# Hybrid RG-LRU / attention block on one core: the merge products as seven half-size products, with token sums made by accumulating transfers

## The chip, the core and the metric

The kernel runs on one core of a Trainium2 chip as one program. A core has TensorE (PE, matrix products), VectorE (DVE), ScalarE (ACT), GpSimd (POOL) and SyncE (SP), each with an instruction stream of its own; they meet through semaphores. Data moves by transfers that an engine issues into its own DMA queue and that run on the core's 16 DMA engines. The metric is the device time of one execution in microseconds (us); lower is better.

## The reference, cut to what matters

One layer over 1024 tokens of 1024 channels, all in float32:

```
y_rnn  = h_x * gelu(gx)                      # scan branch, (1024, 1024)
y_na   = neighborhood_attention(...)         # attention branch, (1024, 1024)
merged = sigmoid(g_rnn) * (y_rnn @ w_rnn_out) + sigmoid(g_na) * (y_na @ w_na_out)
x = x + mx[2] * (merged @ w_out)
x = x + mx[5] * conv_ffn(modulate(x, norm_ffn_g, mx[3], mx[4]), w_up, conv_w, conv_b, w_down)
```

`mx` is the modulation, `silu(c) @ w_mod + b_mod`, in six parts of 1024 columns. Parts 0 and 1 go into the first norm, part 2 is the merge's gate, 3 and 4 shift and scale the second norm, 5 is the gate of the last sum.

## The kernel before, in words

Channels lie on the 128 partitions, tokens along the rows; `KC = 8` chunks of 128 channels make up 1024. `HALF` is 512 tokens or columns. A float32 product is made of three passes: each operand is split into a high part (a cast on ACT) and a low part (raw minus high, on DVE), and PE adds high x high, high x low and low x high into a PSUM bank. PE's unit of work is a matmul with 128x128 stationary weights and 128x512 moving tokens.

The stages in order, with their place in the trace:

- Setup, 0 to 94 us.
- Eight mixer turns (`PAIRS = 8`, one per 128 channels and two heads), 140.5 us each: the projections, the scan, the attention. Each turn stores a chunk of the scan branch to `yr_d` (512 KB), four pieces of the attention branch to `yn_d`, and the two gates' sigmoids to `smr_d` and `smn_d`. POOL does the small exchanges (`exchange_low`), the last step of each sigmoid and the bias adds.
- The merge, 1215 to 1472 us: three phases (`w_rnn_out`, `w_na_out`, `w_out`), each with eight units, one per 128 output channels. A unit is 2 halves x 8 chunks x 3 passes = 48 matmuls. ACT and DVE split the unit's 512 KB of weights; the tokens (`ah`, `al`) are held split in SBUF for the whole phase. In phase 1 DVE multiplies by the gate, adds and splits the merged rows for phase 2. POOL loads one row of gates (`aux`) per unit when DVE frees a buffer. Between the units DVE also makes 32 modulation columns (`mod_column`, L1610: one 128x1024 product with a running sum each; L1613 adds the bias). 24 of the 1152 matmuls already run in the last mixer turn (`mix_piece`), where ACT and DVE also split the eight chunks of `yr_d` (`y_high`, `y_low`) and the first two units of weights.
- The tail of the merge and the second norm, to about 1500 us: `last_unit`, `last_step` and `sum_squares`/`spread` are woven so that PE has work while the norm's short chain runs.
- The feed-forward up products to 1912 us, most of them already made as seven half-size products per pair of 1024-wide blocks. POOL makes the sums of weights that these need by transfers that add into DRAM (L2111, `accum_op=ALU.add`; L2113 are its plain copies).
- The down projection, 1912 to 2127 us: 77 steps of 12 matmuls, also as seven products. SP loads each step's weights and tokens eight steps ahead (`STEP_RING = 8`).

The order of the work is written out by hand on each engine; nothing plans it at run time.

## Time and profile before

| | |
|---|---|
| median of 3 runs | 2131.67 us (2128.15 to 2136.17) |
| profiled execution | 2128.76 us, its span 2126.9 us |
| granted TensorE clock | 0.997 |
| PE busy | 2051.1 us (96%), 10618 matmuls |
| DVE busy | 1628.0 us (77%) |
| ACT busy | 1072.5 us (50%) |
| POOL busy | 492.8 us (23%) |
| DMA | 241.65 MB, mean 114 GB/s |

The profile is of one execution. Its page gives busy time by engine, the span in 40 slices (a digit is the busy tenth of a slice), the chain of work that ended last and the costliest groups of instructions. The rows further down come from that page and from views of the same trace: windows (busy time of each engine in a stretch), lines (groups of instructions by source line), sources (one line's instructions, and for transfers the time from issue to landing) and timelines (single instructions, with the idle time before each in square brackets and what ended it).

### The profile page before, as it was taken

What the parts mean: (1) busy time and instruction counts of PE and PEld (TensorE: products, weight loads), DVE (VectorE), ACT (ScalarE), POOL (GpSimd) and SP (SyncE); (2) the same over time, 40 slices, a digit from 0 to 9 for tenths busy, and PEclk for the clock granted to TensorE, in tenths of its full rate; (3) what the DMA queues carried; (4) which work ended last, traced back from release to release, by engine and by line L of the source; (5) the groups of instructions that cost most, each with busy time, mean ns of one, the idle gap of its engine ahead of it and who ended that gap; (6) DMA issues with size and microseconds to landing.
All of it is one profiled execution on the core that took longest, in us unless ns stands there. A gap on an engine that the chain in (4) does not pass through costs nothing.

```text
span 2126.9 us, 28320 instructions
## 1 busy us (share of the span) xinstructions
PE 2051.1 (96%) x10618; PEld 1739.8 (82%) x10618; DVE 1628.0 (77%) x2809; ACT 1072.5 (50%) x1631; POOL 492.8 (23%) x377
## 2 busy tenths in 40 slices
PE   5999999999999999999998899999999999999999
PEld 1878888988988889888887788887788888887887
DVE  6688598596885985859859866767998888877766
ACT  3466666665676657656666621002444334434332
POOL 0031130222212212212123010000124442115550
PEclk9999999999999999999999999999999999999999
DMA  8421211112012120120111385453347764239663
GB/s 328 112 64 41 62 51 47 47 53 70 30 41 72 40 73 20 53 70 30 43 50 69 106 310 193 144 188 131 89 134 197 183 176 118 94 122 335 226 205 126
DMA packets 105576, 241.65 MB, mean 114 GB/s; under 512 B 27264, under 2 KB 32768, under 8 KB 104960
## 3 DMA queue, kind: packets, MB, share of 16 engines
q1 hardware_dynamic: 74304, 191.08, 26.4%
q0 software_dynamic: 14592, 44.05, 8.0%
q10 hardware_dynamic: 16544, 4.72, 1.0%
q8 instruction: 84, 1.38, 0.3%
q14 instruction: 52, 0.43, 0.1%
HBM read 203.11 MB, written 63.96 MB: 126 GB/s over the span
## 4 chain that ended last, share of the span: by engine, by line
PE 77%; DVE 13%; ACT 4%; issue 2%; ACTq 0%; DVEq 0%
PE banks L47 14%; PE banks L49 14%; PE banks L48 14%; PE banks L991 4%; PE banks L862 4%; PE banks L864 4%; PE banks L863 4%; PE banks L895 3%; PE banks L2269 3%; PE banks L2270 3%; PE banks L2271 3%; DVE probT_low L1494 2%; PE banks L953 2%; DVE prob L1486 2%; PE banks L935 1%
## 5 line engine op out<-in xcount | busy, mean ns | idle before, releaser
L47 PE MATMUL banks<-qh,xnh 128*128 128x384 f32 (+1 forms) x640 | 223.3, 349 | 0.3 <-PEq L216 0.3
L862 PE MATMUL banks<-xnh,wh 128*128 128x512 f32 (+1 forms) x536 | 211.3, 394 | 3.2 <-ACT stage L1097 2.9
L49 PE MATMUL banks<-qh,xnl 128*128 128x384 f32 (+1 forms) x640 | 207.7, 325 | 0.0
L48 PE MATMUL banks<-ql,xnh 128*128 128x384 f32 (+1 forms) x640 | 207.6, 324 | 0.0
L864 PE MATMUL banks<-xnh,wl 128*128 128x512 f32 (+1 forms) x536 | 204.5, 381 | 0.0
L863 PE MATMUL banks<-xnl,wh 128*128 128x512 f32 (+1 forms) x536 | 204.1, 381 | 0.0
L1494 DVE TENSOR_TENSOR probT_low<-banks,probT_high 128x512 fp32r<-128x512 f32 (+2 forms) x256 | 138.9, 583 | 56.2 <-ACT probT_high L1165 55.2
L1165 ACT CAST probT_high<-banks 128x512 fp32r<-128x512 f32 (+2 forms) x256 | 117.0, 510 | 60.3 <-PE banks L953 51.4
L47 PE MATMUL banks<-yh,wh 128*128 128x512 f32 x372 | 145.0, 390 | 0.9 <-DVE wl L2471 0.9
L48 PE MATMUL banks<-yl,wh 128*128 128x512 f32 x372 | 145.0, 390 | 0.0
L49 PE MATMUL banks<-yh,wl 128*128 128x512 f32 x372 | 144.9, 390 | 0.0
L1362 DVE TENSOR_REDUCE ssq<-sqs 128x4 f32<-128x256 f32 (+1 forms) x80 | 31.0, 389 | 141.5 <-ACT sqs L1107 141.0
L803 POOL TENSOR_TENSOR stage<-stage,one 128x512 f32<-128x512 f32 x32 | 39.0, 1217 | 417.8 <-ACT stage L1097 417.8
L813 POOL TENSOR_TENSOR rstd<-rstd,power 128x24 f32<-128x24 f32 (+1 forms) x16 | 58.9, 3680 | 312.3 <-DVE rstd L1400 312.3
L2106 POOL TENSOR_TENSOR conv_d<-conv_d 128x1024 f32<-128x1024 f32 x22 | 69.1, 3141 | 262.8 <-ACT conv_d L2340 201.0
L1155 ACT ACTIVATE prob<-prob,stat 128x768 f32<-128x768 f32 (+1 forms) x128 | 128.2, 1002 | 2.5 <-DVE stat L1489 2.5
L47 PEld LDWEIGHTS banks<-qh,xnh 128*128 128x128 f32 x640 | 120.8, 189 | 9.0 <-issue 8.1
L48 PEld LDWEIGHTS banks<-ql,xnh 128*128 128x128 f32 x640 | 120.8, 189 | 8.3 <-issue 7.6
L49 PEld LDWEIGHTS banks<-qh,xnl 128*128 128x128 f32 x640 | 120.7, 189 | 0.0
L1780 ACT CAST wh<-raw 128x1024 fp32r<-128x1024 f32 x22 | 23.2, 1055 | 189.4 <-PE banks L49 158.9
L864 PEld LDWEIGHTS banks<-xnh,wl 128*128 128x128 f32 x536 | 101.3, 189 | 19.7
L862 PEld LDWEIGHTS banks<-xnh,wh 128*128 128x128 f32 x536 | 101.7, 190 | 17.3 <-issue 3.0
(396 smaller groups left out, 6015.9 us busy)
## 6 DMA issues: line engine op xcount, KB each, us to landing
raw<-w_ff SPq DMA_DIRECT2D x33, 512.0 KB, 5.7
down_d<-w_down POOLq DMA_DIRECT2D x66, 256.0 KB, 6.9
raw<-w_fm SPq DMA_DIRECT2D x32, 512.0 KB, 6.7
extras<-h_d SPq DMA_DIRECT2D x55, 256.0 KB, 3.9
raw<-w_qkv SPq DMA_DIRECT2D x24, 512.0 KB, 3.9
raw<-w_mix SPq DMA_DIRECT2D x24, 512.0 KB, 4.8
h_d<-conv_d SPq DMA_DIRECT2D x21, 512.0 KB, 3.2
raw<-w_modT SPq DMA_DIRECT2D x16, 512.0 KB, 4.6
```

Of the source, the lines that this page charges most:

```text
L47: pe.matmul(out, w_hi(k), x_hi(k), start=(k == 0), stop=False)
L48: pe.matmul(out, w_hi(k), x_lo(k), start=False, stop=False)
L49: last = pe.matmul(out, w_lo(k), x_hi(k), start=False, stop=(k == chunks - 1))
L862: pe.matmul(out, fh[:, s, k, :], xnh[:, k, c0:c1], start=(k == 0), stop=False)
L863: pe.matmul(out, fh[:, s, k, :], xnl[:, k, c0:c1], start=False, stop=False)
L864: return pe.matmul(out, fl[:, s, k, :], xnh[:, k, c0:c1], start=False, stop=(k == KC - 1))
L895: pe.matmul(f_bank(j)[:, 0:c1 - c0], lw[:, 2 * (n // 3) + d, :], xc[:, c0:c1], start=True, stop=True).then_inc(f_full, 1)
L991: last = pe.matmul(dst, vS[:, s, h, :], moving, start=(n == 0 and part == 0), stop=(n == len(blocks) - 1 and part == 1))
L1155: act.activation(p, p, ACT.Exp, bias=stat[:, u, 1:2], scale=-1.0, accum_out=stat[:, u, 2:3]).then_inc(exp_done, 1)
L1165: act.copy(probT_blocks(pth, u, bank), probT_bank(u, bank)).then_inc(pt_hi, 1)
L1494: dve.tensor_tensor(probT_blocks(ptl, u, bank), probT_bank(u, bank), probT_blocks(pth, u, bank).bitcast(F32), ALU.subtract).then_inc(pt_lo, 1)
L2106: pool.tensor_tensor(ca, ca, cg, ALU.mult).then_inc(gated, 1)
```

## The change

**The products.** Each of the three 1024x1024 merge products is cut into four half-size blocks of weights and tokens and made as seven half-size products, in the order `LEFT`, `RIGHT`, `SUM_2`, `SUM_3`, `SUM_1`, `CORNER`, `SUM_4`. Each product has four steps of 12 matmuls, so the merge has 3 x 28 = 84 steps and 1008 matmuls. A step loads 256 KB of weights and 256 KB of tokens side by side into one of 8 raw buffers, ACT and DVE split them together as one 128x1024 tile, and the split goes into one of 6 slots (`slot_released`: the split of step s waits until PE is done with step s - 6). DVE combines the products from PSUM (`combine`) and gates them (`gate_block`).

**The sums.** Four of the seven products need sums of blocks. Sums of the weights (`mix_d`, 96 transfers of 256 KB) are made by POOL's queue in turns 1 to 6, three groups a turn. Sums of the tokens (`sum_d`, 32 transfers for each phase) are made by the same queue: those of the scan branch in turns 4 to 7, eight transfers in six dependent rounds for each row of four, those of the attention branch in phase 0 of the merge (rounds of 8, 8, 4, 4, 4 and 4), those of the merged rows in phase 1 as the rows come out (12 copies, 12 adds and copies, 4 adds), and after the last merged row 4 adds that `SUM_2` needs and 12 adds for the rest.

**The columns.** Of the 32 modulation columns, 24 go into mixer turns 1 to 6 (four a turn, one ahead of each `head_squares`), and the eight of the last gate into steps 16 to 23 of the down projection; their rows (512 KB each) are loaded by SP there.

**The rest.** The scan and attention branches are stored with a sign for half of their blocks (`rnn_out` and `outputs`). In the last turn four splits of merge steps stand where ten splits of rows and weights stood, and eight pieces of 3 matmuls (`left_piece`) where `mix_piece` stood. In the tail ACT makes the squares and POOL most of the adds into `total`; the norm's order of rows is changed and `root(0)` stands behind the first two weight casts. POOL loads no gates in the merge any more; SP and ACT do.

The diff at its core:

```diff
+            def weight_sums(j):
+                if issued[0]:
+                    pool.wait_ge(mix_sums, 16 * issued[0])
+                for step in range(len(SUM_STEPS)):
+                    ...
+                    if step == 0:
+                        sum_into(ph, 0, k, a21, False)
+                        sum_into(ph, 2, k, a11, False)
+                    elif step == 1:
+                        sum_into(ph, 0, k, a22, True)
+                        sum_into(ph, 2, k, a21, True)
+                    ...
                     exchange_low(i, 1, 0)
+                    if not first:
+                        weight_sums(3 * i - 3)
                     sigmoid(i, F_MR, 0, 4)
...
                 for s in range(4):
+                    if not first and not last:
+                        modulation(4 * i - 4 + s)
                     head_squares(i, s)
...
-                    if last and u % 2 == 1 and u >= 5:
-                        mix_piece((u - 5) // 2)
+                    if last and u in (5, 7, 9, 11):
+                        left_piece(3, (u - 5) // 2)
...
+            def load_step(s):
+                g, ph, p, k = of(s)
+                sp.wait_ge(step_lo, s - STEP_RING + 1)
+                ...
+                if k == 0 and p == SUM_2:
+                    if ph < 2:
+                        sp.wait_ge(token_sums, 16 * 32 * (ph + 1))
+                    else:
+                        sp.wait_ge(mix_sums, 16 * (8 * 3 * KC // 2 + 4))
+                elif k == 0 and p == SUM_3 and ph == 2:
+                    sp.wait_ge(token_sums, 16 * (64 + 28 + 12))
+                ...
+            pool.wait_ge(merged, 8)
+            then()
+            for k in range(4):
+                pool.dma_start(sum_d[2, 1, k], mg[:, k, high], accum_op=ALU.add).then_inc(mix_sums, 16)
+            for n in (2, 0, 3):
+                for k in range(4):
+                    sum_into(n, k, mg[:, k, high], True)
+            for r in (1, 2, 3):
+                total_add(r)
...
+            for g in range(1, 19):
+                for k in range(4):
+                    pe.wait_ge(step_lo, 4 * g + k + 1)
+                    for m in range(4):
+                        times(pe, 4 * g + k, m)
...
+                if 16 <= s < 16 + KC:
+                    n = s - 16
+                    ...
+                    mod_column(dve, 5 * KC + n, n % 2, gate_rows[:, n, :], silu_row, gate_dots, bm, mod, gate_dotted,
+                               merge_mod, GATE_DONE + n + 1)
```

Three places show how the instructions move. First DVE, towards the end of phase 1 of the merge. Before, a unit's rows come one after another (`aux` and `x` are the gate product and the merged rows, `yh` and `yl` their split for phase 2, `wl` the split of the next weights):

```order
L1831 TENSOR_TENSOR aux<-banks,aux 128x512 [waits c_full]
L1834 TENSOR_TENSOR x<-x,aux 128x512 [waits c_part]
L1804 TENSOR_TENSOR wl<-raw,wh 128x1024 [waits c_raw_in1,c_w_hi,c_free]
L1853 TENSOR_SCALAR yh<-x 128x512
L1856 TENSOR_TENSOR yl<-x,yh 128x512 [waits c_merged_hi]
L1853 TENSOR_SCALAR yh<-x 128x512
L1856 TENSOR_TENSOR yl<-x,yh 128x512 [waits c_merged_hi]
```

In the changed kernel, steps 60 to 65, with L2136 the low split of a step, L2169 the combining of the last product of phase 1, and L2176 with L2183 the gate product and the merged pair of rows:

```order
L2136 TENSOR_TENSOR wl<-mix_raws,wh 128x1024 [waits c_step_in5,c_step_hi]
L2169 TENSOR_TENSOR blocks_c<-held_products,banks 128x1024 [waits c_merged,c_combined,c_gated,c_product]
L2136 TENSOR_TENSOR late_operands<-mix_raws,late_operands 128x1024 [waits c_step_in6,c_step_hi]
L2169 TENSOR_TENSOR blocks_c<-held_products,banks 128x1024 [waits c_merged,c_combined,c_gated,c_product]
L2136 TENSOR_TENSOR late_operands<-mix_raws,late_operands 128x1024 [waits c_step_in7,c_step_hi]
L2176 TENSOR_TENSOR blocks_c<-blocks_c,aux 128x1024 [waits tokens_in7,c_combined]
L2183 TENSOR_TENSOR merged<-merged,blocks_c 128x2x512 [waits c_gated]
L2176 TENSOR_TENSOR blocks_c<-blocks_c,aux 128x1024 [waits tokens_in5,c_combined]
L2183 TENSOR_TENSOR merged<-merged,blocks_c 128x2x512 [waits c_gated]
L2136 TENSOR_TENSOR late_operands<-raw,late_operands 128x1024 [waits c_step_in0,c_step_hi]
```

The last two merged pairs stand behind the low split of step 63; the split below them is that of step 64, the first that takes sums of merged rows.

Second POOL, over the same stretch. Before it only loads gates (`aux`, L1723) there:

```order
L1723 DMA aux<-smn_d 128x1024 [waits c_free] x8
```

In the changed kernel it issues the sums of merged rows (L1943 copies, L1941 and L1985 add):

```order
L1941 DMA sum_d<-merged 128x512 [waits c_token_sums,c_merged]
L1941 DMA sum_d<-merged 128x512 x3
L1985 DMA sum_d<-merged 128x512 [waits c_token_sums,c_merged]
L1985 DMA sum_d<-merged 128x512 x3
L1941 DMA sum_d<-merged 128x512 x12
L1952 TENSOR_TENSOR total_x1<-total_x1,aux 128x512 [waits c_squared]
```

The four of L1985 wait for the last merged pair and for all earlier sums; the load of step 64 waits for them, that of step 68 for the twelve behind.

Third POOL in a mixer turn. Before, the exchanges of the keys (L795) are followed at once by the sigmoid (L803, L806):

```order
L795 TENSOR_TENSOR kX<-kS,one 64x512 [waits b_low_exchanged,b_tr_lo,b_rms_root]
L795 TENSOR_TENSOR kX<-kS,one 64x512 [waits b_low_exchanged]
L803 TENSOR_TENSOR stage<-stage,one 128x512 [waits b_f_free,b_low_exchanged]
L806 TENSOR_TENSOR stage<-stage,half_one 128x512 [waits b_shifted]
```

In the changed kernel, turn 2 (L838 are the exchanges, L846 and L849 the sigmoid, L866 and L864 the copies and adds into the weight sums `mix_d`):

```order
L838 TENSOR_TENSOR kX<-kS,one 64x512 [waits b_low_exchanged,b_tr_lo,b_rms_root]
L838 TENSOR_TENSOR kX<-kS,one 64x512 [waits b_low_exchanged]
L866 DMA mix_d<-w_mix 128x512 [waits c_mix_sums]
L866 DMA mix_d<-w_mix 128x512
L864 DMA mix_d<-w_mix 128x512 x2
L866 DMA mix_d<-mix_d 16x4096
L864 DMA mix_d<-w_mix 128x512
L846 TENSOR_TENSOR stage<-stage,one 128x512 [waits b_f_free,b_low_exchanged]
L849 TENSOR_TENSOR stage<-stage,half_one 128x512 [waits b_shifted]
```

Six transfers now stand between the exchange and the first sigmoid of the turn.

## Rows read from the trace of the kernel before

**Rows 1.** The page: busy time by engine (first figure PE); granted clock by slice.
```profile
PE 2051.1 (96%) x10618; PEld 1739.8 (82%) x10618; DVE 1628.0 (77%) x2809; ACT 1072.5 (50%) x1631; POOL 492.8 (23%) x377
PEclk9999999999999999999999999999999999999999
```

**Rows 2.** Windows: stretch, length, busy PE, PEld, DVE, ACT, POOL, clock, DMA share, GB/s.
```profile
1060.00:1215.00 155.00, 138.63 (x813) 120.69 (x812) 122.64 (x260) 103.60 (x174) 32.11 (x21) 1.00 0.20 65
1215.00:1296.00 81.00, 81.00 (x359) 67.13 (x358) 47.79 (x77) 17.73 (x18) 10.28 (x18) 1.00 0.78 277
1296.00:1384.00 88.00, 88.00 (x390) 72.90 (x389) 59.24 (x97) 8.45 (x8) 4.30 (x8) 1.00 0.48 162
1384.00:1472.00 88.00, 88.00 (x396) 73.04 (x395) 56.36 (x91) 11.26 (x13) 8.57 (x16) 1.00 0.49 161
1472.00:1560.00 88.00, 85.63 (x373) 68.20 (x372) 82.85 (x102) 43.17 (x55) 16.39 (x15) 1.00 0.36 107
1912.00:2127.00 215.00, 210.08 (x925) 173.02 (x923) 153.17 (x134) 81.97 (x91) 92.05 (x56) 1.00 0.65 225
1912.00:1935.00 23.00, 21.94 (x98) 17.78 (x97) 19.69 (x11) 8.14 (x9) 16.80 (x10) 1.00 0.98 345
1935.00:1960.00 25.00, 24.42 (x107) 19.90 (x108) 18.70 (x13) 14.85 (x17) 6.96 (x4) 1.00 1.03 374
```

**Rows 3.** Timeline of POOL in phase 1, start, duration: two gate loads, one per unit.
```profile
1320.61 0.54 POOL L1723 DMA_DIRECT2D aux<-smn_d  x1 [10.34 <-DVE x L1834]
1331.49 0.54 POOL L1723 DMA_DIRECT2D aux<-smn_d  x1 [10.34 <-DVE x L1834]
```

**Rows 4.** Lines of DVE in the merge: count, busy us, mean ns, idle before.
```profile
L1804 DVE TENSOR_TENSOR wl<-raw,wh 128x1024 fp32r<-128x1024 f32 x22 | 26.9, 1223 | 8.4 <-ACT wh L1780 8.2
L1610 DVE CUSTOM_DVE_ANT_0 row_c<-row_c,sc 128x1024 f32<-128x1024 f32 x16 | 19.5, 1220 | 2.2 <-DMA row_c<-w_modT 2.1
L1613 DVE TENSOR_TENSOR mod<-dots_c,bm 128x1 f32<-128x1 f32 x32 | 5.1, 159 | 1.1
L1844 DVE TENSOR_TENSOR total_x<-total_x,square_c 128x512 f32<-128x512 f32 x12 | 8.3, 692 | 0.4
```

**Rows 5.** Lines of ACT in the merge.
```profile
L1780 ACT CAST wh<-raw 128x1024 fp32r<-128x1024 f32 x22 | 23.2, 1055 | 189.4 <-PE banks L49 158.9 <-DMA raw<-w_mix 20.6 <-PE banks L1753 9.8
```

**Rows 6.** Source L2111, POOL's adding transfers of 256 KB: all 44, issue to landing.
```profile
L2111 POOL DMA_DIRECT2D down_d<-w_down x44: 809/1166/1877, 1530.6 to 1809.0; - x44
DMA to landing us min/median/max: 4.2/8.3/12.8
```

**Rows 7.** Timeline of POOL from 1615 us, start, duration: eight transfers of one batch.
```profile
1615.34 1.09 POOL L2113 DMA_DIRECT2D down_d<-w_down  x2
...
1619.05 1.82 POOL L2111 DMA_DIRECT2D down_d<-w_down  x1
```

**Rows 8.** Landing of that batch: its first transfer; its sixth and eighth (adds).
```profile
DMA to landing us min/median/max: 4.0/4.0/4.0
...
DMA to landing us min/median/max: 10.7/11.5/12.2
```

**Rows 9.** Source L1730, POOL's four plain stores of 256 KB: issue to landing.
```profile
DMA to landing us min/median/max: 2.3/2.3/5.6
```

**Rows 10.** Source L2037, SP's 256 KB loads of down steps: issue to landing.
```profile
DMA to landing us min/median/max: 2.4/3.5/9.0
```

**Rows 11.** Timeline of DVE in a mixer turn: the last wait for the heads' squares.
```profile
535.88 0.42 DVE L1362 TENSOR_REDUCE ssq<-sqs 128x4 f32<-128x256 f32 x1 [6.96 <-ACT sqs L1107]
```

**Rows 12.** Timeline of POOL in the same turn: exchange, then first sigmoid.
```profile
571.49 2.15 POOL L795 TENSOR_TENSOR kX<-kS,one 64x512 fp32r<-64x512 f32 x2 [0.17 <-POOL kcX L795]
585.20 1.04 POOL L803 TENSOR_TENSOR stage<-stage,one 128x512 f32<-128x512 f32 x1 [11.55 <-ACT stage L1097]
```

**Rows 13.** Timeline of POOL from 1598 us: a transfer's issue, and the next one's.
```profile
1598.12 1.21 POOL L2113 DMA_DIRECT2D down_d<-down_d  x1
1609.99 0.81 POOL L2111 DMA_DIRECT2D down_d<-w_down  x1 [10.65 <-issue]
```

More of the change, by code:

```diff
@@ L721, in turn @@
                     store_y(i - 1, 3)
+                if not first and not last:
+                    load_mod_row(4 * i - 2)
+                    load_mod_row(4 * i - 1)
                 if first:
@@ L1523, in turn @@
                 for s in range(4):
+                    if not first and not last:
+                        modulation(4 * i - 4 + s)
                     head_squares(i, s)
@@ L1894 @@
 ONTO_A = (LEFT, SUM_2, SUM_1, SUM_4)
-ORDER_NORM = (0, 4, 1, 5, 2, 6, 3, 7)
+ORDER_NORM = ((0, 1, 2, 3, 4, 5, 6, 7), (4, 5, 6, 7, 0, 1, 2, 3))
 BANKS_A, BANKS_D = (5, 4, 6, 7), (2, 0, 1, 3)
-def ffn_programs(nc, sem, sbuf, w_ff, w_down, ffn_p, mod, total, gain, ones, ident, eps, x1, ops, xh, xl, outT, x1_d,
+MIX_STEPS = 28
+MIX_LAST = 3 * MIX_STEPS
+SLOTS = 6
+AUX_RING = 3
+BLOCK_PRODUCTS = (RIGHT, SUM_1, CORNER, SUM_4)
+BLOCK_OF = {p: n for n, p in enumerate(BLOCK_PRODUCTS)}
+SQUARES = (0, 1, 2, 3, 8, 9, 10, 11, 4, 5, 6, 7, 12, 13, 14, 15)
@@ new lines, with add_token_sums, sum_into @@
+SQUARE_SLOT = {1: 1, 2: 2, 3: 3, 8: 0, 9: 4, 10: 5, 11: 1, 5: 2, 6: 3, 7: 0, 12: 4, 13: 5, 14: 1, 15: 2}
+POOL_ADDS = (1, 2, 3, 8, 9, 10, 5, 6, 7, 12, 13)
+DVE_ADDS = (11, 14, 15)
+def add_token_sums(pool, y_d, out_d, done, before, rows):
+    low, high = slice(0, HALF), slice(HALF, T)
+    issued = [before]
+    def sum_into(n, k, src, add):
+        issued[0] += 1
+        if add:
+            pool.dma_start(out_d[n, k], src, accum_op=ALU.add).then_inc(done, 16)
+        else:
+            pool.dma_start(out_d[n, k], src).then_inc(done, 16)
+    for step in range(6):
+        if step:
+            pool.wait_ge(done, 16 * issued[0])
+        for k in rows:
+            if step == 0:
+                sum_into(0, k, y_d[k, :, high], False)
+                sum_into(2, k, y_d[k, :, high], False)
+            elif step == 1:
+                sum_into(0, k, y_d[k, :, low], True)
+                sum_into(2, k, y_d[KC // 2 + k, :, high], True)
+            elif step == 2:
+                sum_into(1, k, out_d[0, k], False)
+            elif step == 3:
+                sum_into(1, k, y_d[KC // 2 + k, :, high], True)
+            elif step == 4:
+                sum_into(3, k, out_d[1, k], False)
+            else:
+                sum_into(3, k, y_d[KC // 2 + k, :, low], True)
@@ L1900, in ffn_programs @@
+def ffn_programs(nc, sem, sbuf, w_ff, w_down, ffn_p, w_modT, c_rows, bm, mod, gate_rows, silu_row, total, gain, ones, ident, eps, x1, ops, xh, xl, outT, x1_d,
                  h_d, down_d, down_sums, tokens_in, step_raws, weights, every, merge_over, ffn_first):
```

944 lines of the change are left out of this document (594 added, 350 removed).

## The prediction, written before the changed kernel ran

> **What bounds the kernel now.** I read the page first: PE is busy 96% of the span at full clock, so this is a PE-bound program, and what it is given less to do shortens it as long as its operands arrive [rows 1]. Then the windows, one per stage [rows 2]. In the merge, from 1215 to 1472 us, the busy time of PE equals the length of each stretch: nothing in it waits. DVE is busy 47.8 of 81, 59.2 of 88 and 56.4 of 88 us, ACT far less. Only the first stretch moves much data, 277 GB/s at a DMA share of 0.78. The last mixer turn leaves PE idle for 155.0 - 138.6 = 16.4 us, and the stretch with the second norm for 2.4 us. The start of the down projection runs at a DMA share of 0.98 and 1.03 with 345 and 374 GB/s, and there PE keeps up almost wholly. Half a per cent, about 10.7 us, is what a measurement of this kernel can tell from no change.
>
> **What the products remove.** A unit of 48 matmuls takes 1331.49 - 1320.61 = 10.88 us [rows 3], so a matmul takes 0.2267 and a step of 12 takes 2.72. The merge goes from 1152 to 1008 matmuls: 144 x 0.2267 = **-32.6 us**. That is all the change can give in PE time.
>
> **What the steps ask of the others.** A step needs a 128x1024 cast on ACT, 1.05 us [rows 5], and a low split on DVE, 1.22 us [rows 4]. DVE adds a combining operation of the same shape in half of the steps (1.22) and in phases 0 and 1 gate products, so with 50 operations for the 28 steps of phase 0 and 58 for those of phase 1 it averages 2.2 and 2.5 us for a step of 2.72. It keeps up within a phase, but it is no longer far ahead: with six slots the low split of step s ends only about when PE ends step s - 4. The loads are 512 KB a step, 188 GB/s by themselves. Up to the load of step 36, about 85 us after the start, there are 14.7 MB of steps, 4.2 of gates, 4.2 of x and 8.4 of sums of `yn`: 31.5 MB or 370 GB/s, as much as the 374 seen [rows 2], so transfers of this phase run late. The sums of `yn` may take these 85 us. Their rounds (8, 8, 4, 4, 4, 4) at 4.2 us for the first landing [rows 6] and 1.5 for each further one are 6 x 4.2 + 26 x 1.5 = 64 us, plus 5 until they start: in time, with 16 us to spare.
>
> **The seam between phases 1 and 2** is where I put most of the loss. `SUM_2` of the last product takes sums that need the last merged row. Steps 56 to 63 need only rows that are there, so PE works on; by the order of DVE (low split of 63, then two gate pairs of some 2.5 us) the last merged pair comes about 0.7 us before PE ends step 63. Only then are the four adding transfers issued. Such a transfer took 4.2 to 12.8 us, median 8.3 [rows 6]; a batch of eight issued in 4 us landed over (1619.05 + 12.2) - (1615.34 + 4.0) = 11.9 us, or 1.7 apart [rows 7, 8]. Here SP's loads stand still behind the same wait, so I take the smallest landing and 1.5 apart: the fourth lands after 4.2 + 3 x 1.5 = 8.7. The load of step 64 follows, 3.5 at the median [rows 10] and 1.4 for its second half and for the adds still under way, then two casts and the taking of bank pair 0, 3 x 1.05. PE starts step 64 at -0.7 + 8.7 + 4.9 + 3.2 = 16.1 us late, and 0.8 more is lost on pair 1. The load of step 68 waits for all sixteen adds: 4.2 + 15 x 1.5 = 26.7, then 3.9 to load, a cast and three DVE operations of 1.22 (4.7) before the product behind can have its bank. That is 34.6 - 0.7 = 33.9 against the 16.9 + 10.9 = 27.8 at which PE gets there: 6.1 more, and 2.5 for the second pair. Together **+25.5**. Lower end: the sums behave like POOL's plain stores, 2.3 us [rows 9] and spaced as issued, 0.54. Then the fourth lands at 3.9, the load takes 2.4, and the stall is -0.7 + 3.9 + 2.4 + 3.2 + 0.8 = 9.6, with no second one (sixteen land at 10.4). Upper end: 2.4 apart, where it is 40 (worked out below).
>
> The Trainium skill, "DMA: Bandwidth & Descriptors", section "Anatomy of one DMA — SWDGE (gpsimd) path", fits a transfer from this queue as 2.0 us plus its bytes over 436 GB/s, an estimate of 2.6 us for 256 KB. The plain stores agree (2.3), the adding ones do not (4.2 at least), and the page tells no price for adding; by 2.6 and issues 0.54 apart the stall would be the lower end, a rival below.
>
> **The smaller terms.**
> - *Merge start*: `take(0, 0)` stands behind the load of step 8: +0.7; between 0 and 3.
> - *Last turn*: ten casts and ten low splits become four, 6 x 1.05 us less on ACT and 6 x 1.22 less on DVE [rows 4, 5], in a stretch where PE waits 16.4 us for these two. Most of the waits are on the attention's own chain, so I take a third of DVE's 7.3: -2.5; between -5 and 0.
> - *Norm tail*: four last sums, squares on ACT and `total` adds on POOL, where a 128x512 operation takes 1.04 [rows 12] against 0.69 on DVE [rows 4], stand ahead of the norm's chain, in a stretch where DVE is busy 83 of 88 us [rows 2]: +3; between 0 and 6.
> - *Down projection*: nine more 512 KB loads, 4.7 MB, meet a queue at 345 to 374 GB/s: 13 us of backlog. Loads are issued eight steps, 21.8 us, ahead, which covers the 13 and a landing of 3.5 with 5 to spare. Eight columns of 1.38 us on DVE, busy 153 of 215, are hidden. +0.5; between 0 and 5.
> - *Mixer turns*: a column is a product of 1.22 us and a bias add of 0.16 [rows 4], four a turn. They stand before `head_squares`, where DVE waits for ACT, the last time 6.96 us [rows 11]: hidden; without that cover 5.5 us a turn. On POOL six transfers come between exchange and sigmoid, where it was idle for 11.55 us [rows 12]; at 0.54 for a copy and 1.2 for an add (the median in [rows 6]) they take 4.3. But a transfer's issue once stood for 10.65 us behind a full queue [rows 13]; then the sigmoid is late by 10.65 + 4.3 - 11.55 = 3.4. Each batch waits for the earlier one to land, so the queue is empty when it starts. +1; between 0 and 20 (six turns of 3.4).
> - The 24 columns gone from the merge free DVE, which PE did not wait for: 0.
>
> **Sum**, against the profiled execution of 2128.8 us: -32.6 + 25.5 + 0.7 - 2.5 + 3 + 0.5 + 1 = **-4.4**, that is 2124.4. The median shown is 2131.7, by 2.9 above it, and the profile fell near the low end of 2128.2 to 2136.2; from the median the sum gives 2127.3. I take **2126**.
>
> **The rivals.**
> - *A, the sums land quickly.* The seam costs 9.6 to 15 us. For it: the adds come alone, with SP's queue standing, and the stores of SBUF rows took 2.3 [rows 9]. Against it: no adding transfer took under 4.2. At the lower end 25.5 - 9.6 = 15.9 less: 2110; half of the way is 2118. By the Trainium skill's fit above (same page and section) this case would be the one; the adding rows speak against it, so it gets no more than its row's share.
> - *B, POOL's queue is slow (slower than before).* One mechanism: adds land 2.4 us apart or more. In favour: the median of 8.3 and the maximum of 12.8 [rows 6], and a DMA share of 0.78 in this part already [rows 2], to which the steps add. At 2.4 the fourth add lands at 11.4 and PE starts step 64 at 18.8; the sixteenth lands at 40.2, its block of banks is ready at 48.1 against 30.5, and the seam costs 0.8 + 18.8 + 17.6 + 2.5 = 39.7. The sums of `yn` take 6 x 4.2 + 26 x 2.4 + 5 = 93 us against 85: +8. Together 2126 + 14.2 + 8 = 2148. It decides for slower (over 2142.3) from about 2.2 apart.
> - *C, the queue fills in the mixer turns.* 10.65 us for an issue in all six turns: +20 less the 1 in the sum, 2145. Against it: that stall came behind five transfers in 2 us with others under way, and here each batch starts on an empty queue.
> - *D, the gain shows in full*, 2105 or less, because the stall hides in something I have not seen. Nothing in the order supports it.
>
> **Chances.** The forecast's case, adds 1.2 to 2.0 apart, 0.46, with a range of its own from 2117 to 2136; A 0.27; B 0.14; C 0.07; D 0.06. Below 2121 (faster) lie A and D, and 0.09 of the first: 0.42. Above 2142.3 lie most of B and C: 0.19. Between them 0.39. The range 2107 to 2146 leaves out D and the far half of B.
>
> **What would show it right or wrong.** In the profile after: PE busy lower by 32 to 33 us; PE idle in the merge in one place, before the first matmul of step 64, for 16 us, released by a chain of SP load, adding transfer and the last merged row; a second wait of 6 to 9 us some 11 us later. L1985 with a first landing near 4 us and 1.5 apart. Step 36 not waiting. The idle of PE in mixer turns 1 to 6 as before, 2 to 3 us a turn; POOL's first sigmoid in a turn still waiting for ACT. The last turn's idle near 14 us, the norm's near 5. It is wrong if PE waits at the start of each product within a phase (DVE or loads too slow for 2.72 us a step), if step 36 waits, or if the mixer turns get longer than 140.5 us.

## The result, and the profile after

The changed kernel takes 2200.07 us (median of 4 runs, 2198.26 to 2201.82) against 2130.77 us before: 1.0321 of the time, 95% interval 1.0308 to 1.0334. It is slower by 69 us where 2126 was forecast.

By stage, from the starts of the first and last matmuls of each in the two timelines (us):

| | before | after | |
|---|---|---|---|
| setup and turns 0 to 4, to the start of turn 5 | 798.9 | 799.1 | +0.2 |
| turns 5 and 6 | 140.5, 138.3 | 150.4, 147.7 | +19.3 |
| last turn | 137.4 | 141.6 | +4.2 |
| merge and tail, to the first feed-forward matmul | 257.4 | 296.2 | +38.8 |
| second norm and strips | 439.4 | 442.9 | +3.5 |
| down projection | 215.0 | 218.7 | +3.7 |

The page answers to [rows 1]. PE has its 144 matmuls less and is still busy almost as long, since a part of them ran at the lower clock:

```profile
PE 2049.3 (93%) x10474; PEld 1726.7 (79%) x10474; DVE 1731.8 (79%) x2815; ACT 1137.4 (52%) x1704; POOL 661.3 (30%) x553
PEclk9999999999999999999999999979999999999999
DMA  8411324153451562351214499894246774229673
```

The windows answer to [rows 2]: stretch, length, busy time of PE, PEld, DVE, ACT, POOL, granted clock, DMA share, GB/s. Where nothing waited in the merge before, 1440 to 1460 us now holds one matmul, at clock 0.50, with the DMA engines full:

```profile
797.00:840.00 43.00, 36.80 (x184) 31.13 (x183) 22.29 (x27) 21.80 (x33) 14.86 (x8) 0.92 0.47 139
1340.00:1360.00 20.00, 8.66 (x32) 6.91 (x33) 7.88 (x7) 8.01 (x8) 0.00 (x0) 0.74 0.93 326
1420.00:1440.00 20.00, 12.46 (x43) 9.71 (x42) 8.21 (x7) 2.09 (x2) 9.08 (x14) 0.82 0.78 133
1440.00:1460.00 20.00, 0.37 (x1) 0.40 (x2) 2.45 (x2) 3.00 (x3) 11.03 (x13) 0.50 1.10 226
1460.00:1480.00 20.00, 16.09 (x53) 12.16 (x53) 8.23 (x8) 8.51 (x9) 0.00 (x0) 0.76 0.92 272
2025.00:2050.00 25.00, 21.26 (x92) 16.74 (x91) 23.42 (x35) 10.49 (x16) 10.70 (x7) 1.00 0.71 253
```

PE's timeline shows where it waited (start, duration; idle before it and what ended it, in brackets). The first two rows are step 12, the next three step 36 and the matmuls behind it, then the second half of step 60, step 64, the splits of steps 82 and 83, the norm, and the down projection:

```profile
1269.88 0.77 PE L2022 MATMUL banks<-wh 128*128 128x512 f32 x1 [2.97 <-DVE blocks_c L2156]
1270.87 0.63 PE L2024 MATMUL banks<-wh,wl 128*128 128x512 f32 x1
1351.34 0.77 PE L2022 MATMUL banks<-wh 128*128 128x512 f32 x1 [11.74 <-ACT held_products L2074]
1351.90 0.63 PE L2023 MATMUL banks<-wl,wh 128*128 128x512 f32 x1
1352.33 0.63 PE L2024 MATMUL banks<-wh,wl 128*128 128x512 f32 x1
1423.85 0.79 PE L2022 MATMUL banks<-wh 128*128 128x512 f32 x1 [3.84 <-DVE blocks_c L2169]
1459.63 0.77 PE L2022 MATMUL banks<-late_operands 128*128 128x512 f32 x1 [23.34 <-ACT held_products L2074]
1517.97 0.56 PE L2022 MATMUL banks<-late_operands 128*128 128x512 f32 x1 [2.87 <-DVE late_operands L2136]
1521.27 0.79 PE L2022 MATMUL banks<-late_operands 128*128 128x512 f32 x1 [1.88 <-DVE late_operands L2136]
1537.89 0.47 PE L2523 MATMUL banks<-yh,wh 128*128 128x512 f32 x1 [2.17 <-DVE yl L2856]
2045.77 0.50 PE L2606 MATMUL banks<-wh 128*128 128x512 f32 x1 [2.65 <-DVE wl L2993]
```

Merge and tail last 296.2 us; their 984 matmuls at 0.2267 us are 223.1. Of the 73 us between, 54 are idle times like these, and the rest, 17 to 19, is the lower of TensorE's two clocks: after a wait the matmuls start 0.43 us apart (1351.90 to 1352.33) in place of 0.23. This loss does not grow in step with the wait: it was 3.1 us behind the wait of 2.97, 1.6 behind 11.74, and 8.6 in the whole seam from step 60 on.

**The mixer turns.** In turns 5 and 6 PE's first wait leads to ACT (in turn 7 it is 2.0 us for a small load, `lw`, and ACT's comes later). In the timeline of ACT the second square of the turn waits for the store of the last attention rows, which share their place in SBUF with the squares; before, it waited for nothing there:

```profile
810.50 0.28 ACT L1201 ACTIVATE sqs<-banks 128x128 f32<-128x128 f32 x1 [6.70 <-DMA yn_d<-yT]
```

In the timeline of DVE the scan chain is slow behind it:

```profile
824.12 5.22 DVE L1461 SCALAR_TENSOR_TENSOR gD<-gD,gR 128x1280 f32<-128x1280 f32 x1
```

The view of that store's source line gives its time to landing: 12.8 us at 797.7, where it was 2.1 us in the kernel before. It was issued behind three loads of 512 KB for the products, as before, and now also behind two modulation rows and `silu(c)`. Without the sums (no_scan_sums below) it landed in 6.1 and 7.2 us in turns 5 and 6, without the rows (rows_left_out) in 7.9 both times, so each of the two delays it. That agrees with the Trainium skill, "DMA: Bandwidth & Descriptors", section "Queues, rings and completion order": on each DMA engine the descriptors of SP's queue are consumed in the order of the queue. POOL's timeline shows what runs beside both:

```profile
787.61 1.11 POOL L1754 DMA_DIRECT2D sum_d<-yr_d  x2
794.74 1.73 POOL L1752 DMA_DIRECT2D sum_d<-yr_d  x2 [6.02 <-DMA sum_d<-yr_d]
805.96 0.52 POOL L1754 DMA_DIRECT2D sum_d<-sum_d  x1 [9.49 <-DMA sum_d<-yr_d]
811.82 0.80 POOL L1752 DMA_DIRECT2D sum_d<-yr_d  x1 [5.34 <-DMA sum_d<-sum_d]
819.64 1.02 POOL L900 TENSOR_TENSOR bias<-bias,cst 128x256 f32<-128x256 f32 x1
822.81 5.19 POOL L907 TENSOR_TENSOR bias<-bias,cst 128x1792 f32<-128x1792 f32 x1
```

The rounds of the scan branch's sums keep POOL from the bias adds until 819.6; before, they started at 796.7. Now they run beside DVE's operation of 128x1280, which takes 5.22 us where it took 1.49.

**The sums of the attention branch** answer to [rows 6 to 8]. Their second round in POOL's timeline, and the last transfers:

```profile
1264.64 5.92 POOL L1752 DMA_DIRECT2D sum_d<-yn_d  x7 [13.01 <-DMA sum_d<-yn_d]
1285.03 0.81 POOL L1752 DMA_DIRECT2D sum_d<-yn_d  x1 [14.46 <-issue]
1335.74 1.68 POOL L1752 DMA_DIRECT2D sum_d<-yn_d  x2 [8.75 <-issue]
```

The view of source L1752 for the seven adds of 1264.64 gives their time to landing:

```profile
DMA to landing us min/median/max: 7.4/11.8/17.0
```

The first lands at 1272.1, the seventh, issued at 1267.9, at 1284.8: 2.1 us apart. The eighth is not issued before. The last of all lands at 1341.5, and step 36 was due at 1339.6.

**The seam.** The chain of waits from 1426 us on, start, duration, what, is the whole stall in one view:

```profile
1426.10 1.24 DVE merged L2183
1427.33 0.28 issue
1427.61 1.62 POOL sum_d L1941 x2
1429.23 7.08 DMA sum_d<-merged
1436.36 0.47 issue
1436.83 1.62 POOL sum_d L1985 x2
1438.44 7.40 DMA sum_d<-merged
...
1448.92 12.54 DMA raw<-sum_d
```

The last merged pair is done at 1429.7, but POOL still waits for the round of the pair before. Its four adds are issued at 1436.8 and have landed at 1445.9, in 9.0 us. The loads behind them take until 1453.5 for the first token half.

### The profile page after: what moved, and what is told of

It reads as the page before. It is cut to its first block, busy times and chain, and to the rows that moved or that the text cites. A ratio compares the mean times of both kernels' runs of the same rounds, so it can differ in the third digit from the quotient of the medians.

```text
span 2196.5 us, 28675 instructions
## 1 busy us (share of the span) xinstructions
PE 2049.3 (93%) x10474; PEld 1726.7 (79%) x10474; DVE 1731.8 (79%) x2815; ACT 1137.4 (52%) x1704; POOL 661.3 (30%) x553
## 4 chain that ended last, share of the span: by engine, by line
PE 59%; DVE 17%; DMA 6%; issue 6%; ACT 5%; POOL 2%; SPq 0%; DVEq 0%; ACTq 0%; POOLq 0%
PE banks L47 10%; PE banks L49 10%; PE banks L48 10%; PE banks L1081 4%; PE banks L952 3%; PE banks L954 3%; PE banks L953 3%; PE banks L985 3%; PE banks L2606 2%; PE banks L2608 2%; PE banks L2607 2%; DMA sum_d<-yn_d 2%; DVE probT_low L1592 2%; PE banks L1043 2%; DVE prob L1584 1%
## 5 line engine op out<-in xcount | busy, mean ns | idle before, releaser
L846 POOL TENSOR_TENSOR stage<-stage,one 128x512 f32<-128x512 f32 x32 | 40.3, 1258 | 324.8 <-ACT stage L1191 324.8
L2022 PE MATMUL banks<-late_operands 128*128 128x512 f32 x208 | 84.5, 406 | 33.7 <-ACT held_products L2074 24.3
L1081 PE MATMUL banks<-probT_high,vS 128*128 128x256 f32 x448 | 114.0, 293 | 0.0
L953 PEld LDWEIGHTS banks<-xnl,wh 128*128 128x128 f32 x536 | 102.4, 191 | 13.9
L1081 PE MATMUL banks<-probT_low,vS 128*128 128x256 f32 x448 | 108.4, 281 | 0.0
L48 PE MATMUL banks<-tl_d,operands 128*128 128x512 f32 x248 | 98.3, 397 | 0.0
```

The source lines that it names most:

```text
L48: pe.matmul(out, w_hi(k), x_lo(k), start=False, stop=False)
L953: pe.matmul(out, fh[:, s, k, :], xnl[:, k, c0:c1], start=False, stop=False)
L1081: last = pe.matmul(dst, vS[:, s, h, :], moving, start=(n == 0 and part == 0), stop=(n == len(blocks) - 1 and part == 1))
L2022: pe.matmul(out, hi[:, m, :], line(hi)[:, high], start=(k == 0), stop=False)
```

## The experiments

Each kernel was timed against the one before on the same chip; the chips differ from batch to batch, and the median of the kernel before lay between 2129.7 and 2131.0 us on them. All start from the changed kernel unless said otherwise.

| | us | ratio to before, 95% |
|---|---|---|
| no_scan_sums | 2170.89 | 1.0173 to 1.0203 |
| rows_left_out | 2200.08 | 1.0311 to 1.0349 |
| split_wait | 2194.18 | 1.0282 to 1.0325 |
| merged_left_out | 2168.14 | 1.0160 to 1.0190 |
| sums_next_turn | 2177.40 | 1.0205 to 1.0239 |
| pool_adds | 2189.34 | 1.0258 to 1.0289 |
| gate_left_out | 2197.55 | 1.0299 to 1.0330 |
| three_mended | 2155.50 | 1.0099 to 1.0130 |
| seam_on_pool | 2143.31 | 1.0045 to 1.0075 |
| best | 2143.52 | 1.0046 to 1.0070 |
| copies_for_adds | 2185.88 | 1.0249 to 1.0280 |
| no_token_sums | 2111.92 | 0.9901 to 0.9929 |
| yn_early | 2132.95 | 0.9998 to 1.0016 |
| tail_on_dve | 2130.66 | 0.9988 to 1.0006 |

**no_scan_sums** and **rows_left_out** ask what lengthens turns 5 to 7.

```diff
-                        add_token_sums(pool, yr_d, sum_d[0], token_sums, 8 * (i - 4), (i - 4,))
```

> Leaves out the 32 transfers that sum the scan branch's tokens in turns 4 to 7; phase 0 reads unsummed rows there. Theory 1 (these transfers, issued at the end of a turn, hold up the store of the last attention rows, whose landing went from 6 to 7 us to 12.8, 11.5 and 6.1, and keep POOL from the next turn's bias adds until 819.6 instead of 796.7, so that they run beside DVE's scan chain): turns 5 and 6 are 140.5 us again, the last turn as short as before, about -23 us against the changed kernel, some 2177. Rival 1 (the rows of the modulation columns, loaded ahead of that store, are what lengthens the turns): turns 5 to 7 stay 5 us or more too long, over 2185. Both: nothing changes in the seams of the merge.

```diff
-                    load_mod_row(4 * i - 4)
-                    load_mod_row(4 * i - 3)
...
-                mod_column(dve, 2 * KC + q, q % 2, mod_rows[q % 2][:, :], silu_c, col_dots, bm, mod, ...)
```

> Leaves out the loads of the 24 modulation rows and of silu(c) in turns 1 to 6 and the 24 products on DVE (24 tiny bias adds stay). Theory 1: the store of the last attention rows lands in 2 to 6 us, so the first wait in turns 5 and 6 goes, but POOL's bias adds still start 20 us late beside DVE's scan chain (3.7 us of the 10 a turn), so -8 to -16 us. Rival 1: all of the 23 us of the mixer turns go, 2177 or less. Were the columns a cost by themselves, turns 1 to 4 would get shorter than 140.5 us; I expect they do not.

Without the sums turns 5 and 6 are 140.5 and 138.3 us again, the last 138.0; the whole is 29 us shorter, and its profiled execution 24, of which all before the merge gives 19 and merge and tail give 5. Turns 5 to 7 alone are 23 us shorter; setup and turn 0 took 4 more in this execution. Theory 1 holds. Without the rows the turns are 147.6, 148.8 and 144.3, and the time is the same: both theories missed. The store lands in 7.9 us at turns 5 and 6 and the first wait is gone, but the second, behind POOL's late bias adds, is then 5.3 and 5.9 us long. So the store's wait costs nothing by itself as long as the second stands. No run leaves out the late bias adds alone; that the second wait is theirs is read from the timelines. Turns 1 to 4 are 140.5 us either way, so the columns in the turns cost nothing.

**sums_next_turn** keeps every transfer and moves it.

```diff
+                    if i in (5, 6):
+                        pool.wait_ge(yr_out, 16 * i)
+                        for t in range(3):
+                            token_round([(i - 5, t)])
                     if not first:
                         weight_sums(3 * i - 2)
```

> Computes the same. The eight transfers that sum a row of the scan branch's tokens stand inside the next turn on POOL (three rounds ahead of the second group of weight sums, three ahead of the third) and no longer between a turn's last sigmoid and the next turn's bias adds; rows 2 and 3 in the last turn. Theory 1 (it is the place that costs: the late bias adds and the full queue at the turn's start): turns 5 and 6 are 140.5 and 138.3 us again and the last turn 138 to 141, so -18 to -23 us, 2177 to 2182. Rival 1b (the number of transfers costs, wherever they stand, because they slow the stores and loads of the turn): turns 5 and 6 stay 4 us or more too long.

Turns 5 and 6: 140.5 and 138.3; the last 135.7. It is the place, not the number of transfers. The window of turn 5, 799 to 940 us, in no_scan_sums and in this kernel, differs in DMA and POOL alone:

```profile
799.00:940.00 141.00, 138.57 (x822) 123.11 (x821) 117.50 (x254) 91.36 (x158) 40.94 (x32) 1.00 0.33 95
```

```profile
799.00:940.00 141.00, 138.59 (x824) 123.32 (x824) 117.06 (x252) 91.30 (x158) 46.96 (x41) 1.00 0.41 110
```

**split_wait** and **copies_for_adds** take step 36 apart.

```diff
-                        sp.wait_ge(token_sums, 16 * 32 * (ph + 1))
+                        sp.wait_ge(token_sums, 16 * (32 if ph == 0 else 56))
+                elif k == 0 and p == CORNER and ph == 1:
+                    sp.wait_ge(token_sums, 16 * 64)
```

> Computes the same; the load of step 36 waits for the first 24 transfers of the attention branch's sums instead of all 32, and the load of step 48 for the rest. Theory 2 (PE stood 11.7 us before step 36 only because the wait asks for the last two rounds, which step 48 needs first): the fourth round had landed at 1315.8 and step 36 was due at 1339.6, so that wait goes wholly, with 1.5 us of slow clock: -13 us, 2187. Rival 2 (the queue is saturated, so the load of step 36, no longer held back, runs against the adds and slows all of them and the rows that phase 1 needs): less than half of it.

```diff
-            pool.dma_start(out_d[n, k], src, accum_op=ALU.add).then_inc(done, 16)
+            if before == 32:
+                pool.dma_start(out_d[n, k], src).then_inc(done, 16)
```

> Leaves out the adding in the 16 adding transfers for the attention branch's tokens in phase 0: they are plain copies of the same size in the same rounds. Theory 2b (the adding is what costs: adds of one round land 2.0 us apart, copies 1.0 to 1.1): with rounds of 8, 4 and 4 adds some 15 us sooner the sums are there at 1326 and the wait of 11.7 us before step 36 goes: -11 to -13 us, about 2188. Rival 2b (the queue shares full engines, at 0.98 to 1.08 busy, and would be as late with copies): the landings of these rounds stay 1.6 us or more apart and over half of the wait stays.

With the split wait merge and tail fall from 296.2 to 284.6 us and the wait before step 36 from 11.7 to 1.6 us, with 0.9 more at its second pair of banks. Theory 2 holds for its stage. The whole gained only 6 us: in this execution turns 5 to 7 were 4 us longer than in the changed kernel, though nothing differs there. Over the seven kernels with these turns as they are, or without the modulation rows, their sum lay between 439.6 and 444.0 us, so differences of 4 us in a whole time say little here and the stage is the better measure. With copies the same seven transfers of the second round, issued between 1264.0 and 1267.1, land 1.0 us apart, and all sums are there at 1320.7 instead of 1341.5. Their source line (L1753 there), issue to landing:

```profile
DMA to landing us min/median/max: 5.8/7.2/8.5
```

The wait before step 36 is gone, and merge and tail take 279.5 us. It is the adding that costs, on full engines and otherwise the same load.

**merged_left_out**, **pool_adds**, **three_mended** and **seam_on_pool** are about the seam.

```diff
-            for k in range(4):
-                pool.dma_start(sum_d[2, 1, k], mg[:, k, high], accum_op=ALU.add).then_inc(mix_sums, 16)
...
+                elif ph == 2:
+                    sp.wait_ge(merged, 7 + k // 2)
+                    tokens_at = mg[:, k, high]
```

> Leaves out POOL's 64 transfers that sum merged rows; the four products of the third merge product that take sums read the last merged rows as they are, behind the same last merged pair. Theory 3 (the wait at step 64 is the chain last merged pair, POOL's earlier round, four adds, load, and the second one the twelve adds behind): of 23.3 us idle at step 64 some 7 stay (load 3.9, two casts and a take 3.2), the wait of 2.9 behind it goes, and so does most of the clock lost after it (8.6 us): -20 to -28 us, 2172 to 2180. Rival 3 (DVE is the bound at the seam: it comes to the last merged pair too late by itself): the idle at step 64 stays over 12 us.

```diff
+            for k in range(4):
+                pool.wait_ge(step_lo, 64 + k - STEP_RING + 1)
+                pool.tensor_tensor(tokens_of(64 + k), mg[:, k, low], mg[:, 4 + k, high], ALU.add).then_inc(pool_added, 1)
+            for k in range(4):
+                pool.wait_ge(merged, 7 + k // 2)
+                pool.wait_ge(pool_added, k + 4)
+                pool.tensor_tensor(tokens_of(64 + k), tokens_of(64 + k), mg[:, k, high], ALU.add).then_inc(pool_added, 1)
```

> Computes the same. The token halves of steps 64 to 71 (SUM_2 and SUM_3 of the last product) are made by 12 tensor adds of 128x512 on POOL, straight into the raw buffers; 24 adding or copying transfers go, 24 stay for the later products. Theory 3 (the wait at step 64 is the adding transfers and the load behind them): four adds of 1.0 to 2.0 us take the place of 9 us of transfers and 4 to 5 of load; the idle at step 64 falls from 23.3 to 3 to 6 us, the one behind it goes, and most of the slow clock: -28 to -36 us, 2164 to 2172. Rival 3 (DVE at the seam is the bound, and POOL's adds slow it further): the idle stays over 10 us, 2180 or more.

Without the sums (44 transfers; the expectation counts 64) merge and tail fall by 38.4 us (296.2 to 257.8), and no wait stands at step 64, where the expectation left 7 us; the whole, 2168.1, is 4 under its range. The seam is the sums alone. In six other kernels that keep this seam the wait before step 64 was 20.5 to 28.3 us. pool_adds takes the wait at step 64 away and puts another one behind it, 12.7 us before step 72, the first of `SUM_1`:

```profile
1476.98 0.77 PE L2033 MATMUL banks<-wh 128*128 128x512 f32 x1 [12.73 <-DVE held_products L2173]
```

So neither side had it: the gain was there and was given back, since the eight adding transfers that stayed were issued behind the tensor adds. The three mendings together (its diff is the sum of theirs):

> Computes the same; the sums inside the next turn, the split wait before steps 36 and 48, and POOL's adds for steps 64 to 71, all together. If the three causes are separate the gains add up: -20 (turns) -11.6 (step 36, as its stage showed) -33 (step 64) = -65 from 2200.1, 2135, about the kernel before. If they share one queue, part of it is lost or gained twice: off by 8 us or more.

It came out at 2155.5, 20 us more than that. The turns (25 us shorter than in the changed kernel) and step 36 (waits of 1.8 and 0.9 left) did what their own runs did; the seam did not. POOL's timeline shows why. Two adding transfers stood at their issue until the one before had landed, and the tensor adds waited behind them:

```profile
1384.79 1.74 POOL L1977 DMA_DIRECT2D sum_d<-merged  x2 [12.00 <-DVE merged L2227]
1392.46 0.86 POOL L1977 DMA_DIRECT2D sum_d<-merged  x1 [5.93 <-issue]
1399.63 0.86 POOL L1977 DMA_DIRECT2D sum_d<-merged  x1 [6.31 <-issue]
1400.19 4.03 POOL L2019 TENSOR_TENSOR raw<-merged 128x512 f32<-128x512 f32 x3
```

seam_on_pool, from three_mended, has no transfer that sums merged rows:

```diff
+            for k in range(4):
+                add(mg[:, k, low], mg[:, k, low], mg[:, k, high])
+            for k in range(4):
+                add(mg[:, 4 + k, low], mg[:, 4 + k, low], mg[:, 4 + k, high])
+            for k in range(4):
+                pool.wait_ge(pool_added, 17 + k)
+                add(mg[:, 4 + k, low], mg[:, 4 + k, low], mg[:, k, low])
```

> Computes the same as three_mended, but no transfer sums merged rows any more: 24 tensor adds of 128x512 on POOL make all four token sums of the last product, into the raw buffers of steps 64 to 71 and in place in the merged rows for steps 72 to 79. Theory 3b (what was left at the seam, 8.5 us idle at step 64 and 11.4 at step 73, is POOL standing at the issue of an adding transfer for 5.9 and 6.3 us ahead of its tensor adds, and eight adding transfers that come too late for SUM_1): both waits go but for 2 to 3 us at step 64, and 5 us of slow clock with them: merge and tail from 278 to 255 to 260 us, in all 2133 to 2138. Rival 3c (24 adds on POOL beside DVE's splits cost as much, 2.1 us for each where they meet): merge and tail stay over 266.

Merge and tail take 263.0 us, between the two expectations. (Where the expectations name this stage for three_mended, seam_on_pool and yn_early, they count the last 1.4 us of the last turn with it, so 278 and 264.4 there are 276.6 and 263.0 here.) Both waits are gone, and a new one of 4.5 us stands within step 68, where POOL's adds come beside DVE's splits (2.2 us an add and 2.1 a split in the timeline of three_mended); that they are its cause is read from the timeline, not tested.

**yn_early**, from seam_on_pool, makes three quarters of the attention branch's sums in POOL's gaps of turns 5 to 7.

```diff
+                if i >= 5:
+                    pool.wait_ge(yn_out[0], 32 * i)
+                    pool.wait_ge(yn_out[1], 32 * i)
+                    for t in range(3):
+                        token_round([(1, i - 5, t)])
```

> Computes the same as seam_on_pool, with the sums of rows 0 to 2 of the attention branch made in turns 5, 6 and 7 (three rounds behind the bias adds, three between the two roots of the norm); only row 3, 8 of 32 transfers, stays in phase 0. Theory (the small waits of phases 0 and 1, 7.6 us together between 1299 and 1329, are loads that come late because adding transfers fill the engines; a place in POOL's gaps costs nothing): merge and tail 264.4 to 254 to 258, turns unchanged, 2143 to 2134 to 2137. Rival (16 to 24 transfers more in turns 5 to 7 lengthen them again): turns 5 to 7 over 142 us.

Turns unchanged (140.5, 138.3, 135.7), merge and tail 252.5, 2132.95 us: as expected or 1 us better, and level with the kernel before.

**gate_left_out**, **best** and **tail_on_dve** are about the rest.

```diff
-                    mod_column(dve, 5 * KC + n, n % 2, gate_rows[:, n, :], silu_row, gate_dots, bm, mod, gate_dotted,
-                               merge_mod, GATE_DONE + n + 1)
```

> Leaves out the eight rows of 512 KB, the silu row and the eight 128x1024 products of the last gate in the down projection (tiny bias adds stay). Theory 4 (the eight columns stand between the low splits of steps 16 to 23 and make them late: 1.09 and 2.65 us of idle at 2040 and 2046, with the nine loads of 512 KB ahead of them at a DMA share of 1.02 to 1.04): the down projection is 215.0 us again instead of 218.7, so -3.7 us, 2196. Rival 4 (the sums of weights that come from the strips are late): it stays at 218 to 219.

```diff
-                if 16 <= s < 16 + KC:
+                if 12 <= s < 12 + 2 * KC and s % 2 == 0:
...
+                if s == 83:
+                    scale_part(2)
+                    scale_part(3)
+                    square(act, 9)
```

> seam_on_pool and two changes of order more: ACT casts steps 82 and 83 ahead of the second pair of scaled parts, and in the down projection the last gate's rows are loaded at every second step and the columns made at steps 12, 14, ... 26 in place of 16 to 23. If the waits before steps 82 and 83 (2.9 and 2.3 us) are ACT's order, they go, -4; if the down projection's 3.7 us are the bunching of columns and rows, 2 to 3 of them go. Together 5 to 8 us under seam_on_pool: 2127 to 2132, between 0.998 and 1.001 of the kernel before. Rival: the scaled parts then come later to POOL, and the norm's chain waits for them instead: under 2 us gained in the tail.

```diff
+            corner_last(dve, 3)
+            part_last(dve, 0)
+            total_last(dve, 11)
+            part_last(dve, 1)
```

> Computes the same as yn_early; the four parts of x that POOL adds in the tail (128x1024, after ACT has scaled them) are made by eight fused operations of 0.75 us on DVE, and ACT casts steps 82 and 83 ahead of the rest. Theory 5 (in the tail POOL's adds of 2.4 to 5.2 us slow DVE, whose low split took 3.4 us and whose 128x8 operation took 2.3, and PE waits for these): the waits before steps 82 and 83 (5.2 us) and in the norm (3.5) fall by 4 to 6 us in all: 2129 to 2132, 0.998 to 1.001 of the kernel before. Rival (DVE is full there and 6 us more of its own work cost what they save): within 2 us of yn_early.

Without the last gate's rows and products the down projection is 215.3 us, where the kernels that have them took 218.6 to 221.3: theory 4 holds for its stage (the medians differ by 2.5 us only, with overlapping intervals). Spreading them over twice as many steps gained nothing that shows in this scatter (220.7 against 221.1), so no sign speaks for their bunching; whether the 11 us of DVE time or the 4.7 MB cost more was not told apart. ACT's casts moved ahead took the waits before steps 82 and 83 away and gave back 6.7 us in the norm's chain: the rival held, and none of the 5 to 8 us came (2143.5 against 2143.3).

```profile
1466.76 0.37 PE L2552 MATMUL banks<-ones,total_x 128*128 128x1 f32 x1 [6.69 <-DVE total_x L2160]
```

tail_on_dve shortens merge and tail from 252.5 to 247.5 us and lengthens the norm and the strips from 441.9 to 445.4. At 2130.66 against 2132.95 with overlapping intervals, a small gain cannot be told from the rival (within 2 us). What the tail costs is thus placed, not mended.

**no_token_sums** leaves all token sums and the last gate's columns out and keeps all else.

> The changed kernel without any token sums (scan, attention and merged rows are read unsummed) and without the last gate's rows and products in the down projection. Weight sums, the 24 columns in the turns, the seven products and the tail stay. If token sums and these columns are all that turned the change round, the turns are 140.5 us, merge and tail 257.8 (the run without sums of merged rows) less 11.6 (the wait before step 36) less 5 for smaller waits under full engines, 240 to 243, the norm and the strips 442.5, the down projection 215.3: 2113 to 2119, ratio 0.992 to 0.995. Then 15 us of the 32.6 are still missing, and lie in the tail, the slow clock after waits and the strips. If another cost is in it (weight sums, columns in the turns), it stays over 2125.

Faster than the kernel before by 0.85%: 2111.92 us, merge and tail 238.7, down projection 215.1. Token sums and these eight columns are 88 of the changed kernel's us, more than all that it lost. The weight sums, three times as many adding and copying transfers as for one product's tokens, and the 24 columns in the turns cost nothing that shows: turns 1 to 4 take 140.5 us in the changed kernel too, but for turn 2 with 0.4 more.

## Why the prediction was wrong, point by point

- *The products, -32.6 us.* Right in count and unit (10618 to 10474 matmuls). It shows only where nothing waits: no_token_sums has merge and tail at 238.7 us, 18.7 under before and 14 short of the full term: 8 us of idle, over half of it in the tail, and the rest at the lower clock.
- *Mixer turns, +1, and last turn, -2.5: measured +23.7.* This is the largest miss. The step that failed is "each batch waits for the earlier one to land, so the queue is empty", as if POOL's own queue were the only thing at stake. I weighed the weight sums, which cost nothing, and gave the token sums of turns 4 to 6 no term at all. (An empty queue at its start did not keep a batch of weight sums from standing either: at 746.6 POOL stood 8.3 us behind three transfers of the same batch. But its next sigmoid still waited 11.2 us for ACT.) The token sums stand where the next turn begins: there SP's loads and a small store meet them in the same engines, ACT waits for that store, and the instructions queued behind the waits on POOL (the bias adds) come beside DVE's scan. That queue was not followed. With the sums moved the last turn is 135.7 us, 1.7 under before, where I had 2.5: right in sign and within its range.
- *Sums of the attention branch in time with 16 us to spare: 11.7 us late.* The term was mis-sized: landings 1.5 us apart gave 64 us; adds were 2.0 to 2.1 apart and some stood at their issue for 14.5 and 8.8, and they took 94, from 8.6 us after the merge's start in place of 5. Rival B had the mechanism and nearly the number (93 against 85, +8), with a chance of 0.14. Of what its wait held back, a quarter was not needed yet.
- *The seam, +25.5: measured 23.3 + 3.8 + 1.0 + 2.9 + 0.7 us idle and 8.6 at the lower clock, 40.* The four adds were sized well (8.7, measured 9.0). Left out was the earlier round that POOL must still wait for (7.1). The load took 7.6 us on full engines in place of 4.9, and the two casts and the taking 6.1 in place of 3.2, since the second cast waited 3.0 us for its own load. Against this the last merged pair came 6.6 us ahead of PE's need and not 0.7: -6.6 + 7.1 + 9.0 + 7.6 + 6.1 is the 23.3, within rounding.
- *The clock.* No term priced it. Waits of 3 us and more cost PE some microseconds on top, 17 to 19 in merge and tail. One of these waits, 3.0 us before step 12 with 3.1 at the lower clock behind it, had no term either.
- *Merge start +0.7, norm tail +3, down +0.5.* No wait stands in the merge's first 12 steps. The down projection took 3.7, within its range. The tail had waits of 2.9, 1.9, 1.1 and 2.2 with some 3 to 5 us of slow clock, against 2.4 before; +9 to +11, over the 6 of its upper end. The first of these waits is ACT's order: DVE stood 3.85 us for the cast of step 82, which comes behind the scaled parts, and in `best`, where the casts come ahead of them, the waits before both steps are gone. POOL beside DVE, the reason as given, adds to the later ones, but with adds of 128x1024 and not with the small ones: a low split took 3.37 us beside one, an operation of 128x8 took 2.33.

```profile
1516.80 3.33 POOL L1959 TENSOR_TENSOR x<-x,blocks_c 128x1024 f32<-128x1024 f32 x1
1522.31 5.16 POOL L1959 TENSOR_TENSOR x<-x,held_products 128x1024 f32<-128x1024 f32 x2
```

```profile
1517.84 3.37 DVE L2136 TENSOR_TENSOR late_operands<-mix_raws,late_operands 128x1024 fp32r<-128x1024 f32 x1
1525.16 2.33 DVE L2821 SCALAR_TENSOR_TENSOR gm_d<-mod,gain 128x8 f32<-128x8 f32 x1
```

Three sums of the prediction are off, too little to change the forecast: 26.7 + 3.9 + 4.7 - 0.7 is 34.6 and not 33.9 (0.7 us more of stall), three copies and three adds at its own prices are 5.2 us and not 4.3, and 512 KB in 2.72 us is 193 GB/s and not 188.

What stayed right is the kind of loss, a chain of dependent adding transfers at a seam of two products. What was wrong is that it was looked for in one place; it stood in four, and the range was built around that one.

## What to carry to other kernels

A sum made by adding transfers is cheap where nothing waits for it soon: 96 transfers, half of them adds, cost nothing that shows in the middle of the mixer turns, while 108 others, 60 of them adds, are most of what made this kernel slower by 3%. Before moving such work, list for each place what stands behind it on the issuing engine, which small transfer shares the DMA engines with it and who waits for that one; and let each consumer wait for the part it reads. A gain in PE's work is paid out only if PE does not wait, since a wait of even 3 us was followed by as much again at the lower clock.

## What the runs showed of the hardware

- Adding transfers of 256 KB landed 2.0 to 2.1 us apart when DMA engines were full and 1.3 to 1.4 apart at the seam, with SP's queue standing (1443.1, 1444.4, 1445.9). Copies of the same size landed 1.0 apart on full engines; no run has them alone at the seam.
- POOL can stand at the issue of an adding transfer until an earlier one has landed, with one or two under way (5.9 and 6.3 us) as well as with seven (14.5). A plain copy stood too, 8.2 us behind seven copies, in copies_for_adds.
- POOL's tensor operations beside DVE's slow both: 5.22 us for 1.49, 3.37 for 1.22, 2.33 for 0.16 on DVE, and 5.19 for 4.04 on POOL (the bias add at 822.8). It looks like waiting for each other more than like sharing: POOL's three operations beside those of DVE ended at 828.0, 1520.1 and 1527.5, and DVE's at 829.3, 1521.2 and 1527.5; in three_mended adds of 2.2 us and splits of 2.1 alternate, and 1.04 + 1.22 is 2.26. The Trainium skill, "GPSIMD Engine Reference", section "Specifications", has the two engines share SBUF interfaces, with contention for DVE instructions that have two SBUF inputs; all three here have two, so the trace agrees.
- After a wait of 3.0 us PE's matmuls started 0.43 us apart until 1275.6, and after one of 11.7 us until 1354.5, in a window with a granted clock of 0.74; TensorE's lower level, 1.2 GHz, is 0.50 in that column.
